# Memory tiles normed before the history and the gate weights, the low parts of the memory projection split over two engines, and the laps reordered

## The chip, the cores and the metric

The kernel runs on one core of a Trainium2 chip as one launch. The metric is device time in microseconds (us) of that launch, the median of three runs. A core has five engines that work side by side and meet at semaphores: TensorE (PE; its weight loads are shown as PEld), VectorE (DVE), ScalarE (ACT), GpSimd (POOL) and SyncE (SP), which issues DMAs. Each runs its own list of instructions in order.

## The reference

One step of a hybrid streaming encoder layer in float32. The part that matters here is its beginning: the memory tokens and the frames are normed, and the normed memory is projected to keys and values, which are outputs too.

```python
def rms_norm(x, g):
    y = xf * lax.rsqrt(jnp.mean(xf * xf, axis=-1, keepdims=True) + RMS_EPS)
    return (y * g.astype(jnp.float32)).astype(x.dtype)

def mem_kv(mem, g, w):                       # mem (1, 256, 1024), w (1024, 2048)
    kv = rms_norm(mem, g) @ w
    mk, mv = jnp.split(kv, 2, axis=-1)
...
    xn = rms_norm(x, g_mix_pre)              # 1024 prompt frames and 8 * 16 sample frames
    q, k, v, o, ig, fg, glu, xq, gates = jnp.split(xn @ w_in, IN_SPLITS, axis=-1)
```

Then come a matrix memory (mLSTM), a causal convolution over a stored history, cross-attention into the memory keys and values, a gated merge and a feed-forward block. The change touches none of that.

## The kernel before

Every product of the kernel is made in three: each operand is cut into a high part (a cast to fp32r) and a low part (the operand less its high part), and high times high, high times low and low times high are added up in PSUM. So the weights pass through two engines before TensorE may use them. A **unit** is 128 columns of a weight, 128x1024 numbers: SP loads it into `w_raw` (four buffers), ScalarE casts it to `w_hi` (two buffers, `split_hi`, L262), GpSimd subtracts to get `w_lo` (two buffers, `split_lo`, L266), and TensorE runs 24 matmuls (`use_unit`, L274). ScalarE may write `w_hi` of unit u only when TensorE has used unit u-2 (`w_used`).

The program has phases with a barrier of all engines between them (`end_phase`). The change lies in the first phase, whose five parts are `sp_norm`, `pool_norm`, `act_norm`, `pe_norm` and `dve_norm`. It has a beginning and 16 steps.

**The tiles.** Eleven tiles of 128 rows are normed and turned: 0 and 1 are the memory, 2 the sample frames, 3 to 10 the prompt. For a tile t, ScalarE squares it (`square`, L438, the sum goes to `x_ss`), VectorE makes the variance (first instruction of `scale`, L539, signals `x_var`), GpSimd takes the power -1/2 (`rstd`, L398, signals `x_rstd`), VectorE multiplies (second instruction of `scale`, L543, writes `x_s`), TensorE transposes eight blocks (`turn`, L492), VectorE applies the gain in two halves (`gain`, L549), ScalarE casts the two halves (`hi`, L444), and the low parts are made of half 0 by VectorE (`lo`, L556) and of half 1 by GpSimd (`lo`, L394). There are two buffers of `x_in` and of `x_s`, and `x_T` has one for each half.

**The beginning.** SP issues four weight units, the two memory tiles, seven vectors, the taps of the convolution, the history (`hist_in`, 960 KB) and, once GpSimd has cleared `wif`, the columns of the gate weights (L333). TensorE first transposes vectors, taps and history, then tiles 0 and 1. ScalarE casts two units and the gate weights before it squares a tile; GpSimd does low parts of the two units and of the gate weights ahead of the first `rstd`. The tiles 0, 1 and 2 are scaled and the tiles 0 and 1 gained before the steps begin.

**The steps.** Step j (`body`) runs unit j of the memory projection. In every even step one tile is handled too, with t = 3 + j/2: `scale` of tile t, `gain`, `hi` and `lo` of tile t-1 and, in step j of TensorE, `turn` of tile t-1. The result of a unit is copied from PSUM by ScalarE (`kv_T`, L460), transposed by TensorE (`kv_turn`, L502), copied by VectorE (`kv_nat`, L569) and stored. Two steps with one tile are called a pair here. `kv_steps` writes the first four steps out, and runs the other twelve as a loop of three laps of four steps, in which waits are made against registers.

Of the kernel before, what the change touches and what calls it, by code (L numbers as in the profile page):

```python
# [88 lines left out]
def hybrid_step(nc, a, o):  # L89
    ctx = ExitStack()  # L90
    with ctx:
# [228 lines left out]
        def sp_norm(sp):  # L320
            for s in range(RAW):
                load_w(sp, s, s, w_kv_v[:, :, s * P:(s + 1) * P])
            for t in range(2):
# [35 lines left out]
        def pool_norm(pool):  # L359
            steps = st["pool"] = Steps(pool, pool_steps)  # L360
            pool.sem_inc(x_lo, 1)
            steps.mark(nc.gpsimd.memset(wif[:], 0.0))
# [27 lines left out]
            def lo(t, dst):  # L390
                pool.wait_ge(x_hi, 2 * t + 2)
                d_hi, d_lo = dst(1)
                pool.wait_ge(consts_ready, 1)
                nc.gpsimd.tensor_tensor(d_lo, x_T[:, 1], d_hi.bitcast(F32), ALU.subtract).then_inc(x_lo, 1)  # L394

            def rstd(t, b):
                pool.wait_ge(x_var, t + 1)
# [26 lines left out]
        def act_norm(act):  # L424
            st["act"] = Steps(act, act_steps)
            split_hi(act, 0, 0, 0)
            split_hi(act, 1, 0, 1)
            act.wait_ge(wif_loaded, 32)
            nc.scalar.copy(wif_hi[:], wif[:]).then_inc(wif_hi_done, 1)
# [1787 lines left out]
```

## Time and profile before

| | us |
|---|---|
| median of three runs | 2942.94 (2941.67 to 2944.8) |
| span of the profiled execution | 2940.9 |
| beginning, up to the first matmul of unit 0 | 37.05 |
| first matmul of unit 0 to the first matmul of the second phase | 79.39 |
| PE busy over the span | 2737.7 (93%) |
| DVE, ACT, POOL busy over the span | 1066.5, 791.7, 1043.4 |

The span is measured from the first to the last instruction of one profiled execution; the median lies 2.0 us above it. All times in rows are us from the start of the span. In a row of the timeline the first number is the start and the second the duration; what stands in brackets is how long the engine had been idle, and what ended that. After the first phase TensorE works without a gap for a long time, so what the first phase loses or gains moves the rest.

### The profile page before, as it was taken

To read this page: it belongs to the slowest core of one execution; us is meant where nothing else is said; L and a number is where in the kernel's file an instruction comes from. 1 tells how busy PE (TensorE), PEld (TensorE's weight loads), DVE (VectorE), ACT (ScalarE), POOL (GpSimd) and SP (SyncE) were. 2 spreads that over 40 slices of the span, in tenths; PEclk is the share of its full clock that TensorE was granted. 3 is DMA by queue.
4 is the path that set the end of the run, shared out by engine and by line. 5 is a ranking of instruction groups with operands and counts; after the bars stand their busy time and mean duration, and the time that the engine had idled before them with its cause. 6 is when DMAs were issued, how large, how long until landed. Compare 5 with 4: busy or idle time off the path is not lost.

```text
span 2940.9 us, 41651 instructions
## 1 busy us (share of the span) xinstructions
PE 2737.7 (93%) x15764; PEld 2676.4 (91%) x15764; DVE 1066.5 (36%) x1418; ACT 791.7 (27%) x1172; POOL 1043.4 (35%) x525
## 2 busy tenths in 40 slices
PE   5899999999999998989988989779998899969997
PEld 5899999999999998978788879769997899969997
DVE  3320399999922222156433423231103211041101
ACT  4321111111113323044311410233333333233332
POOL 5411222222211112122011201346665566646664
PEclk9999999999999999999999989989999899989999
DMA  6422333433252232534654435424444244433442
GB/s 174 139 88 92 121 118 112 136 115 108 91 178 89 82 96 100 168 106 117 210 174 167 148 133 187 156 76 123 137 141 136 86 121 139 132 115 114 124 134 78
DMA packets 469265, 372.11 MB, mean 127 GB/s; under 512 B 13626, under 2 KB 437906, under 8 KB 469168
## 3 DMA queue, kind: packets, MB, share of 16 engines
q1 hardware_dynamic: 454264, 317.52, 35.7%
q10 hardware_dynamic: 14912, 53.48, 4.7%
q8 instruction: 46, 0.75, 0.1%
q14 instruction: 43, 0.35, 0.0%
HBM read 285.86 MB, written 85.55 MB: 126 GB/s over the span
## 4 chain that ended last, share of the span: by engine, by line
issue 47%; PE 34%; POOL 14%; DVE 2%; ACT 1%; POOLq 1%; DMA 1%; SPq 0%; DVEq 0%; ACTq 0%
PE PS L274 29%; POOL w_lo L266 12%; PE PS L1504 1%; PE PS L1523 1%; PE PS L1179 1%; PE PS L1187 1%; PE PS L1145 1%; POOL m_lo L1776 1%; DVE x_T L549 0%; POOL m_lo L1987 0%; PE PS L1152 0%; DMA stage<-in_state_conv 0%; DVE y_T L1342 0%; POOL n_r L1971 0%; PE PS L1140 0%
## 5 line engine op out<-in xcount | busy, mean ns | idle before, releaser
L266 POOL TENSOR_TENSOR w_lo<-w_raw,w_hi 128x1024 fp32r<-128x1024 f32 (+1 forms) x324 | 838.1, 2588 | 1434.0 <-ACT w_hi L262 1433.9
L262 ACT CAST w_hi<-w_raw 128x1024 fp32r<-128x1024 f32 (+1 forms) x324 | 356.0, 1099 | 1755.5 <-PE PS L274 1749.0
L274 PE MATMUL PS<-A_hi,w_hi 128*128 128x384 f32 x3024 | 752.4, 336 | 19.0 <-DVE A_lo L948 10.0
L274 PE MATMUL PS<-A_lo,w_hi 128*128 128x384 f32 x3024 | 747.8, 335 | 0.0
L274 PE MATMUL PS<-A_hi,w_lo 128*128 128x384 f32 x3024 | 747.4, 335 | 0.0
L274 PEld LDWEIGHTS PS<-A_hi,w_hi 128*128 128x128 f32 x3024 | 546.2, 189 | 22.9 <-issue 18.0
L274 PEld LDWEIGHTS PS<-A_lo,w_hi 128*128 128x128 f32 x3024 | 546.2, 188 | 0.0
L274 PEld LDWEIGHTS PS<-A_hi,w_lo 128*128 128x128 f32 x3024 | 545.8, 188 | 0.0
L274 PE MATMUL PS<-m_hi,w_hi 128*128 128x384 f32 x1248 | 428.1, 343 | 28.1 <-DVE m_lo L1776 14.9
L274 PE MATMUL PS<-m_lo,w_hi 128*128 128x384 f32 x1248 | 425.7, 341 | 0.0
L274 PE MATMUL PS<-m_hi,w_lo 128*128 128x384 f32 x1248 | 425.4, 341 | 0.0
L903 DVE SCALAR_TENSOR_TENSOR c_out<-ext,taps,c_out 128x1024 f32<-128x1024 f32 x480 | 423.9, 959 | 0.7 <-DVE c_out L903 0.7
L274 PEld LDWEIGHTS PS<-m_hi,w_hi 128*128 128x128 f32 x1248 | 236.8, 190 | 30.2 <-issue 30.0
L274 PEld LDWEIGHTS PS<-m_lo,w_hi 128*128 128x128 f32 x1248 | 236.7, 190 | 0.0
L274 PEld LDWEIGHTS PS<-m_hi,w_lo 128*128 128x128 f32 x1248 | 236.6, 190 | 0.0
L2035 DVE SCALAR_TENSOR_TENSOR ff_tmp<-ff_tmp,PS 128x384 f32<-128x384 f32 x66 | 36.6, 554 | 354.9 <-ACT ff_tmp L1904 354.9
L2018 DVE TENSOR_SCALAR nat<-PS 128x384 f32<-128x384 f32 x48 | 26.6, 557 | 349.2 <-PE PS L1845 349.0
L1027 DVE SCALAR_TENSOR_TENSOR part_out<-gate_in,PS 128x1152 f32<-128x1152 f32 x24 | 32.5, 1355 | 228.6 <-PE PS L274 228.6
L690 ACT ACTIVATE stage<-PS 128x1152 f32<-128x1152 f32 x80 | 89.9, 1124 | 0.0
L2038 DVE SCALAR_TENSOR_TENSOR ff_tmp<-ff_tmp,PS 128x384 f32<-128x384 f32 x66 | 36.6, 554 | 145.1 <-PE PS L274 145.1
L1663 POOL TENSOR_TENSOR A_lo<-xa_T,A_hi 128x512 f32 (+1 forms) x18 | 22.5, 1271 | 140.1 <-ACT A_hi L1619 140.1
L1977 POOL TENSOR_TENSOR A_lo<-ff_tmp,A_hi 128x384 f32 (+1 forms) x66 | 66.9, 1013 | 0.0
(265 smaller groups left out, 2103.5 us busy)
## 6 DMA issues: line engine op xcount, KB each, us to landing
w_raw<-in_w_ffn_in SPq DMA_DIRECT2D x132, 512.0 KB, 3.8
proj_d<-stage ACTq DMA_DIRECT2D x80, 576.0 KB, 2.8
w_raw<-in_w_in SPq DMA_DIRECT2D x80, 512.0 KB, 4.0
w_raw<-in_w_ffn_out SPq DMA_DIRECT2D x48, 704.0 KB, 4.6
gate_in<-proj_d SPq DMA_DIRECT2D x24, 576.0 KB, 6.2
part_d<-part_out SPq DMA_DIRECT2D x24, 576.0 KB, 4.5
w_raw<-in_w_branch SPq DMA_DIRECT2D x24, 512.0 KB, 4.2
w_raw<-in_w_out SPq DMA_DIRECT2D x24, 512.0 KB, 4.0
```

Source lines behind the costliest of these rows:

```text
L262: nc.scalar.copy(w_hi[:, s % SPLIT, 0:kt], w_raw[:, s, 0:kt]).then_inc(w_hi_done, 1)
L266: nc.gpsimd.tensor_tensor(w_lo[:, s % SPLIT, 0:kt], w_raw[:, s, 0:kt], w_hi[:, s % SPLIT, 0:kt].bitcast(F32), ALU.subtract).then_inc(w_lo_ ...
L274: last = nc.tensor.matmul(out, w[:, k], m(k, c), start=start and k == 0 and n == 0, stop=stop and k == kt - 1 and n == 2)
L690: nc.scalar.activation(thirds(stage[:, s % 2]), PS[:, 3 * (s % 2):3 * (s % 2) + 3, 0:TC], func, scale=scale).then_inc(p_copied, 1)
L903: steps.mark(nc.vector.scalar_tensor_tensor(out=c, in0=src, scalar=tap_scalar(w, k), in1=c, op0=ALU.mult, op1=ALU.add))
L1027: nc.vector.scalar_tensor_tensor(out=thirds(part_out[:, s % 2]), in0=thirds(gate_in[:, s % 2]), scalar=1.0, in1=PS[:, 3 * (s % 2):3 * (s % ...
L1145: last = nc.tensor.matmul(PS[:, 0, P * h:P * (h + 1)], k_in[:, b, 2 * h + z], q_in[:, b, 2 * h + z], start=z == 0, stop=z == 1)
L1179: last = nc.tensor.matmul(PS[:, 4 + h, 0:E1], q_in[:, b, 2 * h + z], C_T[:, h, z], start=z == 0, stop=z == 1)
L1187: nc.tensor.matmul(PS[:, 2 * h + z, 0:E1], kw[:, h, P * z:P * (z + 1)], v1[:, h], start=True, stop=True).then_inc(ml_upd, 1)
L1977: nc.gpsimd.tensor_tensor(l, th[:, b], h.bitcast(F32), ALU.subtract).then_inc(f_lo, 1)
L2035: nc.vector.scalar_tensor_tensor(out=th[:, b], in0=th[:, b], scalar=1.0, in1=PS[:, 2 * b, 0:TC], op0=ALU.add, op1=ALU.mult).then_inc(f_v, 1)
L2038: nc.vector.scalar_tensor_tensor(out=th[:, b], in0=th[:, b], scalar=0.5, in1=PS[:, 2 * b + 1, 0:TC], op0=ALU.mult, op1=ALU.mult).then_inc( ...
```

## The change

- `sp_norm` loads the memory tiles first, then two weight units, the vectors, taps and history, and then the other two units.
- GpSimd makes `ident` and `minus_half` alone at the start. The clearing of `wif`, the other constants and the low part of the gate weights come later, so the loads of the gate columns and of tiles 2 and 3, which stand behind them on SP, come later too.
- ScalarE squares tiles 0 and 1 first and casts the gate weights after tile 2's square. TensorE turns tiles 0 and 1 ahead of the history.
- The low part of a unit of the memory projection is made in two halves, one after the other: VectorE does k-blocks 0 to 3 (`kv_low`, signals `kv_lo`), GpSimd blocks 4 to 7 (`kv_low`, waits for `kv_lo`, signals `w_lo_done`).
- In a pair, ScalarE casts the unit before the tile's high parts, VectorE runs `kv_low`, `gain`, `lo` and then `scale` (before: `scale`, `gain`, `lo`), and GpSimd runs `rstd`, `kv_low` and then `lo`. The last lap is written out, and the loop has two laps.

VectorE, steps 2 and 3, written out: before the step begins with the scaling of tile 4 (`x_r`, `x_s`).

```order
L539 TENSOR_SCALAR x_r<-x_ss 128x1 [waits x_sq]
L543 TENSOR_SCALAR x_s<-x_in,x_r 128x1024 [waits x_turned,x_rstd]
L549 TENSOR_TENSOR x_T<-PS,cols 128x512 [waits x_lo0,x_turned]
L549 TENSOR_TENSOR x_T<-PS,cols 128x512 [waits x_lo,x_turned]
L556 TENSOR_TENSOR A_lo<-x_T,A_hi 128x4x128 [waits x_hi]
L569 COPY kv_nat<-PS 128x256 [waits kv_turned]
L569 COPY kv_nat<-PS 128x256 [waits kv_stored0,kv_turned]
```

The same place in the changed kernel:

```order
L567 TENSOR_TENSOR w_lo<-w_raw,w_hi 128x512 [waits w_hi_done]
L582 TENSOR_TENSOR x_T<-PS,cols 128x512 [waits x_lo0,x_turned]
L582 TENSOR_TENSOR x_T<-PS,cols 128x512 [waits x_lo,x_turned]
L589 TENSOR_TENSOR A_lo<-x_T,A_hi 128x4x128 [waits x_hi]
L572 TENSOR_SCALAR x_r<-x_ss 128x1 [waits x_sq]
L576 TENSOR_SCALAR x_s<-x_in,x_r 128x1024 [waits x_turned,x_rstd]
L608 COPY kv_nat<-PS 128x256 [waits kv_turned]
```

The scaling has moved from the first to the last place ahead of the copies of `kv_nat`, and the half low part, which waits for ScalarE's cast of the unit, stands first.

GpSimd, first steps of the loop's lap, before (`x_r` is the power of `rstd`, `A_lo` the tile's low part, rows without tiles are register work and waits):

```order
L398 TENSOR_TENSOR x_r<-x_r,minus_half 128x1 [waits x_var]
L391 ISA
L394 ISA [waits consts_ready,x_hi]
L394 TENSOR_TENSOR A_lo<-x_T,A_hi 128x4x128
L265 ISA
L266 TENSOR_TENSOR w_lo<-w_raw,w_hi 128x1024 [waits w_hi_done]
```

The same place in the changed kernel:

```order
L382 TENSOR_TENSOR x_r<-x_r,minus_half 128x1 [waits x_var]
L385 ISA
L386 TENSOR_TENSOR w_lo<-w_raw,w_hi 128x512 [waits kv_lo]
L376 ISA
L378 ISA [waits x_hi]
L378 TENSOR_TENSOR A_lo<-x_T,A_hi 128x4x128
```

The unit's low part now stands right behind the power, and the tile's low part behind it.

GpSimd at the beginning, before:

```order
L362 MEMSET wif 128x1024
L366 MEMSET ident 128x128 [waits pool_steps]
L366 MEMSET sel 4x512
L366 MEMSET later 128x256
L366 MEMSET own 128x8
L366 MEMSET minus_half 128x4
```

and in the changed kernel:

```order
L368 MEMSET ident 128x128
L369 MEMSET minus_half 128x4
L371 ISA [waits pool_steps]
L371 AFFINE_SELECT ident<-ident 128x128
L382 TENSOR_TENSOR x_r<-x_r,minus_half 128x1 [waits pool_steps,x_var]
L382 TENSOR_TENSOR x_r<-x_r,minus_half 128x1 [waits x_var]
L386 TENSOR_TENSOR w_lo<-w_raw,w_hi 128x512 [waits kv_lo] x2
L378 TENSOR_TENSOR mem_lo<-x_T,mem_hi 128x4x128 [waits x_hi]
L394 MEMSET wif 128x1024
```

The clearing of `wif` has moved behind two powers, two half low parts and the low part of tile 0.

```diff
@@ kv_steps
-            with eng.Fori(1, NKV // RAW) as i:
+            with eng.Fori(1, NKV // RAW - 1) as i:
                 for s in range(RAW):
                     body(RAW * i + s, i, s)
+            for s in range(RAW):
+                body(NKV - RAW + s, NKV // RAW - 1, s)
@@ sp_norm
-            for s in range(RAW):
-                load_w(sp, s, s, w_kv_v[:, :, s * P:(s + 1) * P])
             for t in range(2):
                 sp.dma_start(x_in[:, t], m_src[t]).then_inc(x_loaded[t], 16)
+            for s in range(SPLIT):
+                load_w(sp, s, s, w_kv_v[:, :, s * P:(s + 1) * P])
...
+            for s in range(SPLIT, RAW):
+                load_w(sp, s, s, w_kv_v[:, :, s * P:(s + 1) * P])
             sp.wait_ge(wif_zero, 1)
@@ pool_norm
+            def kv_low(u, s):
+                pool.wait_ge(kv_lo, u + 1)
+                nc.gpsimd.tensor_tensor(w_lo[:, s % SPLIT, KH:KT], w_raw[:, s, KH:KT],
+                                        w_hi[:, s % SPLIT, KH:KT].bitcast(F32), ALU.subtract).then_inc(w_lo_done, 1)
+
+            rstd(0, 0)
+            rstd(1, 1)
+            for s in range(SPLIT):
+                kv_low(s, s)
+            lo(0, lambda h: norm_dst(0, h))
             steps.mark(nc.gpsimd.memset(wif[:], 0.0))
-            pool.wait_ge(pool_steps, 1)
+            steps.wait()
             pool.sem_inc(wif_zero, 1)
+            lo(1, lambda h: norm_dst(1, h))
+            rstd(2, 0)
...
             def body(j, lap, s):
                 if s % 2 == 0:
                     t, b = norm_tile(lap, s)
                     rstd(t, b)
+                if isinstance(j, int) and j + SPLIT >= NKV:
+                    split_lo(pool, j + SPLIT, (s + SPLIT) % RAW)
+                else:
+                    kv_low(j + SPLIT, (s + SPLIT) % RAW)
+                if s % 2 == 0:
                     lo(t - 1, lambda h: norm_dst(t - 1, h))
-                split_lo(pool, j + SPLIT, (s + SPLIT) % RAW)
@@ act_norm
             square(0, 0, 0)
-            for t in range(1, FIRST):
-                square(t, t % 2, t // 2)
-                hi(t - 1, lambda h: norm_dst(t - 1, h)[0])
+            square(1, 1, 0)
+            split_hi(act, 0, 0, 0)
+            hi(0, lambda h: norm_dst(0, h)[0])
+            split_hi(act, 1, 0, 1)
+            hi(1, lambda h: norm_dst(1, h)[0])
+            square(2, 0, 1)
+            act.wait_ge(wif_loaded, 32)
+            nc.scalar.copy(wif_hi[:], wif[:]).then_inc(wif_hi_done, 1)
 
             def body(j, lap, s):
                 if s % 2 == 0:
                     t, b = norm_tile(lap, s)
                     square(t, b, lap + (FIRST + s // 2) // 2)
+                split_hi(act, j + SPLIT, lap + (s + SPLIT) // RAW, (s + SPLIT) % RAW)
+                if s % 2 == 0:
                     hi(t - 1, lambda h: norm_dst(t - 1, h)[0])
-                split_hi(act, j + SPLIT, lap + (s + SPLIT) // RAW, (s + SPLIT) % RAW)
@@ pe_norm
             turn(0, 0)
             turn(1, 1)
+            turn_hist()
...
             pe.wait_ge(x_lo0, FIRST)
             pe.wait_ge(x_lo, FIRST)
+            pe.wait_ge(hist_copied, 4)
@@ dve_norm
+            def kv_low(u, s):
+                dve.wait_ge(w_hi_done, u + 1)
+                nc.vector.tensor_tensor(w_lo[:, s % SPLIT, 0:KH], w_raw[:, s, 0:KH],
+                                        w_hi[:, s % SPLIT, 0:KH].bitcast(F32), ALU.subtract).then_inc(kv_lo, 1)
...
             scale(0, 0)
-            for t in range(1, FIRST):
-                scale(t, t % 2)
-                gain(t - 1, (t - 1) % 2, V_MEM)
-                lo(t - 1, *norm_dst(t - 1, 0))
+            scale(1, 1)
+            vectors()
+            kv_low(0, 0)
+            gain(0, 0, V_MEM)
+            lo(0, *norm_dst(0, 0))
+            kv_low(1, 1)
+            gain(1, 1, V_MEM)
+            lo(1, *norm_dst(1, 0))
+            copy_hist()
+            scale(2, 0)
...
             def body(j, lap, s):
                 if s % 2 == 0:
                     t, b = norm_tile(lap, s)
-                    scale(t, b)
+                if not isinstance(j, int) or j + SPLIT < NKV:
+                    kv_low(j + SPLIT, (s + SPLIT) % RAW)
+                if s % 2 == 0:
                     gain(t - 1, 1 - b, V_MIX)
                     lo(t - 1, *norm_dst(t - 1, 0))
+                    scale(t, b)
```

## Rows read from the trace of the kernel before

**Rows 1.** Busy time by stretch: start:end, length, busy per engine (instructions), clock, DMA, GB/s.

```profile
37.05:116.44 79.39, 63.66 (x483) 60.16 (x481) 29.51 (x57) 39.40 (x64) 52.59 (x32) 0.96 0.61 186
```

**Rows 2.** Timeline of PE: first matmuls of units 0 and 2, and of phase two.

```profile
37.05 0.56 PE L274 MATMUL PS<-mem_hi,w_hi 128*128 128x256 f32 x1
...
45.90 0.35 PE L274 MATMUL PS<-mem_hi,w_hi 128*128 128x256 f32 x1
...
116.44 0.87 PE L274 MATMUL PS<-A_hi,wif_hi 128*128 128x384 f32 x2 [3.16 <-POOLq L284]
```

**Rows 3.** Timeline of DVE, ACT and POOL in the loop, around one pair of steps.

```profile
67.22 0.55 POOL L398 TENSOR_TENSOR x_r<-x_r,minus_half 128x1 f32<-128x1 f32 x1
67.90 0.75 DVE L543 TENSOR_SCALAR x_s<-x_in,x_r 128x1024 f32<-128x1024 f32 x1 [1.53 <-POOL x_r L398]
68.57 1.28 DVE L549 TENSOR_TENSOR x_T<-PS,cols 128x512 f32<-128x512 f32 x2
69.38 1.22 ACT L444 CAST A_hi<-x_T 128x512 f32 x2 [3.19 <-DVE x_T L549]
70.16 0.69 DVE L556 TENSOR_TENSOR A_lo<-x_T,A_hi 128x512 f32 x1 [0.31 <-ACT A_hi L444]
...
72.04 4.70 POOL L266 TENSOR_TENSOR w_lo<-w_raw,w_hi 128x1024 fp32r<-128x1024 f32 x2
```

**Rows 4.** Timeline: a scaling and the turns after it, a cast of a unit, a turn.

```profile
25.07 0.75 DVE L543 TENSOR_SCALAR x_s<-x_in,x_r 128x1024 f32<-128x1024 f32 x1 [0.67 <-POOL x_r L398]
25.88 3.68 PE L492 MATMUL PS<-ident,x_s 128*128 128x128 f32 x16 [2.24 <-DVE x_s L543]
...
42.23 1.05 ACT L262 CAST w_hi<-w_raw 128x1024 fp32r<-128x1024 f32 x1 [3.45 <-PE PS L274]
...
45.02 1.04 PE L492 MATMUL PS<-ident,x_s 128*128 128x128 f32 x8
```

**Rows 5.** Feed-forward phase, timeline around a scaling; then line L2052: duration ns min/median/max.

```profile
1933.59 0.69 DVE L2063 TENSOR_TENSOR m_lo<-u_tail,m_hi 128x512 fp32r<-128x512 f32 x1
1934.42 0.55 POOL L1971 TENSOR_TENSOR n_r<-n_v,minus_half 128x1 f32<-128x1 f32 x1 [2.90 <-DVE n_v L2022]
1934.94 1.28 POOL L1987 TENSOR_TENSOR m_lo<-u_tail,m_hi 128x512 fp32r<-128x512 f32 x1
1935.01 1.77 DVE L2052 TENSOR_SCALAR nat<-x,n_r 128x1024 f32<-128x1024 f32 x1 [0.66 <-POOL n_r L1971]
...
L2052 DVE TENSOR_SCALAR nat<-x,n_r x9: 754/755/1776, 1927.6 to 2633.9; 128x1024 f32<-128x1024 f32 x9
```

**Rows 6.** Busy time by stretch, as in rows 1: three units, and a gap.

```profile
51.93:55.45 3.52, 1.40 (x10) 1.05 (x10) 0.69 (x2) 2.34 (x4) 3.52 (x3) 0.96 0.38 94
55.45:59.93 4.48, 4.48 (x27) 4.48 (x27) 1.71 (x4) 1.22 (x3) 2.79 (x2) 0.65 1.11 351
64.97:67.97 3.00, 3.00 (x27) 3.00 (x27) 0.22 (x2) 1.15 (x2) 2.80 (x2) 1.00 1.07 323
...
102.90:107.51 4.61, 4.61 (x27) 4.61 (x27) 1.84 (x4) 1.37 (x3) 2.79 (x2) 0.63 0.86 266
```

**Rows 7.** Timeline of POOL at the end of the first phase.

```profile
112.29 2.36 POOL L266 TENSOR_TENSOR w_lo<-w_raw,w_hi 128x1024 fp32r<-128x1024 f32 x1
...
114.89 1.43 POOL L394 TENSOR_TENSOR A_lo<-x_T,A_hi 128x512 fp32r<-128x512 f32 x1 [0.24 <-ACT A_hi L444]
```

**Rows 8.** Timeline of the beginning; last a DMA issue: KB, us to landing.

```profile
16.23 0.32 PE L472 MATMUL PS<-ident,vec_in 56*128 56x56 f32 x1 [16.23 <-DMA vec_in<-in_conv_ln_b]
...
29.41 1.06 ACT L438 ACTIVATE sq<-x_in 128x1024 f32<-128x1024 f32 x1 [0.18 <-DMA x_in<-in_x_sample]
...
30.82 0.55 POOL L398 TENSOR_TENSOR x_r<-x_r,minus_half 128x1 f32<-128x1 f32 x1 [0.25 <-DVE x_r L539]
...
35.45 1.94 PE L492 MATMUL PS<-ident,x_s 128*128 128x128 f32 x8 [5.90 <-POOL mem_lo L394]
...
x_in<-in_x_sample SPq DMA_DIRECT2D x1, 512.0 KB, 3.5
```

More of the change, by code:

```diff
@@ L301, in hybrid_step @@
         NKV = 2 * KT
+        KH = KT // 2
         N_IN = NT + MEM // P
@@ L361, in pool_norm, with lo, rstd @@
             pool.sem_inc(x_lo, 1)
+            steps.mark(nc.gpsimd.memset(ident[:], 0.0))
+            steps.mark(nc.gpsimd.memset(minus_half[:], -0.5))
+            steps.wait()
+            steps.link(nc.gpsimd.affine_select(out=ident[:], in_=ident[:], compare_op=ALU.not_equal, fill=1.0, base=0,
+                                               pattern=[[-1, P]], channel_multiplier=1))
+            pool.sem_inc(ident_ready, 1)
+            def lo(t, dst):
+                pool.wait_ge(x_hi, 2 * t + 2)
+                d_hi, d_lo = dst(1)
+                nc.gpsimd.tensor_tensor(d_lo, x_T[:, 1], d_hi.bitcast(F32), ALU.subtract).then_inc(x_lo, 1)
+            def rstd(t, b):
+                pool.wait_ge(x_var, t + 1)
+                nc.gpsimd.tensor_tensor(x_r[:, b:b + 1], x_r0[:, b:b + 1], minus_half[:, 0:1], ALU.pow).then_inc(x_rstd, 1)
+            def kv_low(u, s):
[7 more added lines that the diff above has]
+            lo(0, lambda h: norm_dst(0, h))
             steps.mark(nc.gpsimd.memset(wif[:], 0.0))
-            pool.wait_ge(pool_steps, 1)
+            steps.wait()
             pool.sem_inc(wif_zero, 1)
-            for t, v in ((ident[:], 0.0), (sel[:], 0.0), (later[:], 0.0), (own[:], 1.0), (minus_half[:], -0.5), (ln_eps[:], LN_EPS)):
+            lo(1, lambda h: norm_dst(1, h))
+            rstd(2, 0)
+            for t, v in ((sel[:], 0.0), (later[:], 0.0), (own[:], 1.0), (ln_eps[:], LN_EPS)):
                 steps.mark(nc.gpsimd.memset(t, v))
             steps.wait()
-            steps.mark(nc.gpsimd.affine_select(out=ident[:], in_=ident[:], compare_op=ALU.not_equal, fill=1.0, base=0,
-                                               pattern=[[-1, P]], channel_multiplier=1))
             steps.mark(nc.gpsimd.affine_select(out=sel[:], in_=sel[:], compare_op=ALU.not_equal, fill=1.0, base=0,
@@ L425, in act_norm @@
             st["act"] = Steps(act, act_steps)
[L426 to L429, printed above, removed]
             def square(t, b, lap):
@@ L469, in pe_norm @@
         def pe_norm(pe):
-            pe.wait_ge(consts_ready, 1)
+            pe.wait_ge(ident_ready, 1)
             pe.wait_ge(vec_loaded, 7 * 16)
@@ L476, in pe_norm, with turn_hist @@
             last.then_inc(vec_T, 1)
-            pe.wait_ge(hist_loaded, 16)
-            for n, bank in enumerate((6, 7, 4, 5)):
-                if bank == 5:
-                    pe.wait_ge(vec_copied, 1)
-                for q in range(4):
-                    k = 4 * (n % 2) + q
-                    last = nc.tensor.transpose(PS[:, bank, 120 * q:120 * (q + 1)], hist_in[:, n // 2, k * P:(k + 1) * P], ident[0:120, 0:120])
-                last.then_inc(hist_Tr, 1)
+            def turn_hist():
+                pe.wait_ge(hist_loaded, 16)
+                for n, bank in enumerate((6, 7, 4, 5)):
+                    if bank == 5:
+                        pe.wait_ge(vec_copied, 1)
+                    for q in range(4):
+                        k = 4 * (n % 2) + q
+                        last = nc.tensor.transpose(PS[:, bank, 120 * q:120 * (q + 1)], hist_in[:, n // 2, k * P:(k + 1) * P], ident[0:120, 0:120])
+                    last.then_inc(hist_Tr, 1)
             def turn(t, b):
@@ L558, in dve_norm @@
             scale(0, 0)
-            for t in range(1, FIRST):
-                scale(t, t % 2)
-                gain(t - 1, (t - 1) % 2, V_MEM)
-                lo(t - 1, *norm_dst(t - 1, 0))
+            scale(1, 1)
[8 more added lines that the diff above has]
+            scale(2, 0)
             def kv_out(e, b, before):
```

42 lines of the change are left out of this document (15 added, 27 removed).

## The prediction

> **What bounds the kernel now.** Only the first phase changes, so I read it alone, in the order in which a reader should: first the busy time by stretch, then the starts of TensorE's units, then the timelines of the engines between two units. From the first matmul of unit 0 to the second phase TensorE is busy for 63.66 of 79.39 us [rows 1]. It waits in every pair of steps, and what it waits for is GpSimd. GpSimd's round in the loop is one power (67.22), an idle stretch until the tile's low part can run, and two low parts of units (72.04, 4.70 us for both): 4.82 + 4.70 = 9.5 us for a pair [rows 3]. Six pairs, from unit 2 at 45.90 to unit 14 at 102.90, take 57.0 us, which is 9.5 each [rows 2, 6]. A unit takes 3.00 us and a turn 1.04 [rows 4, 6], so TensorE has work for about 7.4 us of those. Two of the seven pairs after the first run a slow unit, 4.48 and 4.61 us at a mean granted clock of 0.65 and 0.63; at the beginning of each the granted clock is the 1.2 GHz level, not 2.4 [rows 6]. The pair that begins at 55.45 is no longer for that (64.97 - 55.45 = 9.5): GpSimd hides the slow unit.
>
> **The beginning (term A).** The vectors that TensorE needs first come in behind 3.1 MB, four units and two tiles, and it starts at 16.23 [rows 8]. In the changed kernel 2.1 MB stand ahead of them. By bytes that is 16.23 x 4/6 = 10.8; I take 11.9, since the small loads trail. Vectors and taps are turned and copied by about 14.0 (estimate, half-speed turns and four small copies). Then a chain hangs over three engines: half a low part on VectorE (0.65, as the 0.69 of a 128x512 subtraction), the gain (0.7 to the first cast), two casts (1.2), the cast of unit 1 (1.05 + 0.1), VectorE's half (0.7), GpSimd's half (1.26, as m_lo), GpSimd's low part of tile 0 (1.25): 14.0 + 6.95 = 20.95 [rows 3 to 5]. Behind these on GpSimd stands the clearing of `wif`, 1 us, and behind that clearing wait SP's two gate loads and the sample tile: 22.0, plus 1.0 for two issues, plus 3.5 for the tile [rows 8], plus 0.3 behind the gate packets: 26.8. From a square to the power 1.41, from the power to the scaling 0.6, from it to the turn 0.81, from the turn to unit 0 1.60 [rows 4, 5, 8]: 26.8 + 4.4 = **31.2**, against 37.05. So A = -5.9. If the vectors came at 10.8 it would be -7; if the gate loads held SP for two more us, -4. Ends: -9 and -2. The constants and the gate weights' low part, moved behind the power of tile 2, lie under unit 0, since GpSimd's next power cannot come before unit 0 has ended. The history's turns and copies lie under the load of the sample tile.
>
> **The pairs (terms B and C).** Here the new order makes a ring. VectorE's step now begins with a half low part that waits for ScalarE's cast of unit j+2, which waits until TensorE has used unit j. Behind this half on VectorE stand the gain and low part of tile t-1 and then the scaling of tile t; and unit j+2 stands on TensorE behind the turn of tile t. Before, the scaling came first and did not depend on unit j. So from the end of unit j to the start of unit j+2 run, one after the other: to the cast 0.1, cast and hand-over 1.12, half low part 0.63, gain to cast 0.81, cast to VectorE's low part 0.78 [rows 3, 4], that to the power 0.83, power to scaling 0.6 to 0.68 [rows 3, 5], scaling to turn 0.81, turn 0.9 to 1.0 [rows 4]. The sum is 6.6 (6.3 where the steps are written out, where hand-overs are shorter by 0.1; 6.8 in the loop). GpSimd's half low part, 1.26, is not in this sum: it can run while the tile is scaled and turned. But it does not only hide, it gets in the way. It stands right behind the power, its input has been ready for three us, and so it starts as the power ends, a trace ahead of the scaling. The feed-forward phase has the same two neighbours: power to 1934.97, GpSimd's 128x512 subtraction from 1934.94 to 1936.22, VectorE's 128x1024 scaling from 1935.01, and that scaling takes 1.77 us instead of 0.75 [rows 5]. It happened in three of nine, each time that GpSimd was 0.06 or 0.07 us ahead; the other six took 0.75. So the scaling ends 0.95 later (0.55 after GpSimd's half), and a pair takes 3.0 + 6.6 + 0.95 = 10.5 us instead of 9.5.
>
> The Trainium skill, "SBUF — State Buffer", section "Who interferes with whom", says the same as a rule and speaks against this change: VectorE in a two-port mode and GpSimd share a pair of ports, and whoever issues second is blocked until the first has finished. The trace agrees (1.77 against 0.75). Without it terms B and C below would be smaller by 0.95 for each pair.
>
> **B**, the first pair: unit 0 runs at the low clock as before (45.90 - 37.05 = 8.85 held 5.0 of it). Now 5.0 + 6.3 + 0.95 = 12.3, since nothing of tile 3 is done ahead any more: B = +3.4. **C**, six further pairs at 10.5 instead of 9.5: +6.0. Ends: without the collision B is 2.5 and C 0.6; with loop hand-overs 0.3 dearer C is 8.
>
> **The clock (term D).** TensorE now has, between unit j+1 and the turn, only one pair of small transposes in about 3.4 us. Before, in a like stretch ahead of the slow unit at 55.45, it was busy for 1.40 of 3.52 us, and then the granted clock fell [rows 6]. I expect a fall in nearly every pair. Its price is no longer hidden, as unit and turn lie on the ring: a slow unit costs 1.5 to 1.6 (4.48 and 4.61 against 3.00), and a slow turn 0.9 more (1.94 against 1.04) [rows 4, 6, 8]. I take 1.8 for each of seven units: D = +12.6. Ends: 0, and 7 x 2.5 = 17.
>
> The Trainium skill, "TensorE: Matmul & The Clock Gate", section "HAM oscillation — how this bites in real kernels", has it that a wait of that kind that comes in every round lets every round start cold. By the rows of before alone, two falls in seven, D would be 3. No run here shows yet which of the two holds for this ring.
>
> **The end (term E).** From unit 14 to the second phase it took 116.44 - 102.90 = 13.5. The last two units' low parts stay whole, so after unit 14 come: cast and the high part of tile 9 (to 1.7), its low part, variance and power (to 3.1), a whole low part of 2.35, in which the last scaling is caught, and which it ends 0.5 behind, GpSimd's low part of tile 9 (1.25) and the second whole low part (2.35): 9.55. From the end of that one (114.65 in the trace) to the second phase 1.8 [rows 2, 7]. So 3.0 + 11.35 = 14.3: E = +0.8 (0 to 3).
>
> **The sum.** -5.9 + 3.4 + 6.0 + 12.6 + 0.8 = +16.9. The second phase begins at about 133 instead of 116.4, and nothing after it changes. Against the profiled execution that is 2940.9 + 16.9 = 2957.8, and the runs lie 2.0 above their span: **2960**.
>
> **The rivals.** (1) The clock holds better: collisions as forecast, but two falls of seven as before, D = 3: +7.3, 2950. For it: the other five pairs before kept their clock although TensorE waited in each. Against: in the new ring it waits longer and does less meanwhile. (2) No collision, because in the loop register work stands between power and half low part and the scaling gets ahead. Then pairs have 6.6, idle stretches are shorter, and with four falls at 1.6: -5.9 + 2.5 + 0.6 + 6.4 - 0.1 = +3.5, 2946. Against it: in the loop two low parts follow each other without a gap (4.70 for two of 2.35). (3) The other side, faster: the ring is cheaper than its rows. If hand-overs between VectorE and its neighbours shrink as its halves follow each other, so that a pair takes 8.3 us, C = -7, without falls: -5.9 + 1 - 7 - 0.1 = -12, 2931. It decides from a ring of about 5.3 instead of 7.55 us on; only the loss of a cast and of the collision would give that, and both are in every pair. (4) The change does not bring the memory tiles forward, as the sample tile waits behind the gate loads: A near -1, and with the rest 2965.
>
> **How the numbers follow.** Forecast 0.62 (2953 to 2967), rival 1 0.13, rival 2 0.11, rival 3 and other gains 0.10, rival 4 0.04. The range leaves out rival 3, the lower half of rival 2 and a few above: 2945 to 2967. A measurement of this kernel tells about 0.2% (5.9 us) from no change, so 2948.8 and 2937.1 are the limits: slower 0.75 (forecast, rival 4 and most of rival 1), same 0.14 (rival 2, the rest), faster 0.11.
>
> **What would show it.** Unit 0 near 31 (A). Unit starts 12 to 13 us apart in the pairs, with slow units of some 4.5 us (C, D); 10.5 apart with units of 3.0 would be rival 1. Scalings of 1.7 us with GpSimd's half low part beginning just ahead of each (collision); 0.75 is rival 2. Second phase near 133 (sum). Wrong would be the forecast if a turn starts before the cast of the next unit has been through VectorE: then there is no ring.

## The result and the profile after

The changed kernel takes 2956.57 us (median of four, 2956.21 to 2960.88) against 2942.66 (four runs beside it): a ratio of 1.0051, 95% interval 1.0037 to 1.0066. It is slower by 13.9 us. The profiled execution took 2956.49, its span is 2954.7 against 2940.9. The second phase begins at 131.30 instead of 116.44, 14.86 later; 1.0 of that comes back behind it (2823.4 us from there to the end against 2824.4), and I did not follow that up.

Busy time by stretch of the changed kernel, columns as in [rows 1]: the whole loop, the six pairs from unit 2 to unit 14, then single units, a gap with its turn, a piece of a slow unit, and the gaps ahead of units 10 and 14.

```profile
31.79:131.30 99.51, 69.97 (x482) 66.50 (x480) 52.67 (x73) 39.91 (x64) 44.21 (x36) 0.84 0.52 158
44.27:116.16 71.89, 53.16 (x362) 50.57 (x361) 37.73 (x55) 29.80 (x47) 28.25 (x24) 0.85 0.55 167
...
44.27:49.31 5.04, 5.04 (x29) 5.04 (x27) 0.35 (x2) 0.00 (x0) 1.28 (x1) 0.57 0.64 189
57.40:61.09 3.69, 3.69 (x29) 3.69 (x27) 0.26 (x1) 0.00 (x0) 1.28 (x1) 0.80 0.74 210
68.59:73.19 4.60, 4.60 (x30) 4.60 (x28) 1.03 (x2) 0.40 (x2) 1.43 (x2) 0.63 0.76 203
116.16:119.23 3.07, 3.07 (x30) 3.07 (x28) 2.32 (x4) 0.22 (x2) 1.53 (x2) 1.00 0.75 193
...
65.70:69.10 3.40, 1.35 (x12) 1.36 (x13) 3.25 (x3) 2.47 (x4) 3.04 (x3) 1.00 0.28 95
69.20:72.40 3.20, 3.20 (x17) 3.20 (x17) 0.42 (x2) 0.00 (x0) 1.28 (x1) 0.50 0.84 219
...
88.00:92.52 4.52, 1.28 (x10) 1.05 (x11) 3.53 (x6) 3.14 (x6) 3.32 (x3) 1.00 0.18 63
111.98:116.16 4.18, 1.28 (x11) 1.05 (x11) 3.43 (x6) 3.20 (x6) 3.23 (x3) 1.00 0.20 71
```

Against [rows 1] TensorE is busy 6.3 us longer for the same matmuls (69.97 against 63.66) and waits 13.8 us longer (29.54 against 15.73). The longer busy time is the clock: in 65.70 to 69.10 it was busy for 1.35 of 3.40 us, and from 69.20 to 72.40 the granted clock is 0.50, the 1.2 GHz level. The first units of six pairs in a row (units 2, 4, 6, 8, 10 and 12) begin at that level and last 0.6 to 2.0 us longer than the 3.00 of [rows 6]; the seventh (unit 14, 116.16) runs in 3.07 at 1.00.

The longer wait is the ring. Timeline of the changed kernel from the end of unit 4, which releases the cast of unit 6, to the turn ahead of unit 6:

```profile
61.13 1.05 ACT L262 CAST w_hi<-w_raw 128x1024 fp32r<-128x1024 f32 x1 [4.17 <-PE PS L274]
62.21 0.69 DVE L567 TENSOR_TENSOR w_lo<-w_raw,w_hi 128x512 fp32r<-128x512 f32 x1 [4.54 <-ACT w_hi L262]
62.82 1.28 DVE L582 TENSOR_TENSOR x_T<-PS,cols 128x512 f32<-128x512 f32 x2
63.63 1.21 ACT L458 CAST A_hi<-x_T 128x512 f32 x2 [1.46 <-DVE x_T L582]
64.43 0.69 DVE L589 TENSOR_TENSOR A_lo<-x_T,A_hi 128x512 f32 x1 [0.33 <-ACT A_hi L458]
...
65.27 0.55 POOL L382 TENSOR_TENSOR x_r<-x_r,minus_half 128x1 f32<-128x1 f32 x1 [6.58 <-DVE x_r L572]
...
65.78 1.27 POOL L386 TENSOR_TENSOR w_lo<-w_raw,w_hi 128x512 fp32r<-128x512 f32 x1
65.85 1.75 DVE L576 TENSOR_SCALAR x_s<-x_in,x_r 128x1024 f32<-128x1024 f32 x1 [0.66 <-POOL x_r L382]
...
67.75 1.09 PE L514 MATMUL PS<-ident,x_s 128*128 128x128 f32 x8 [2.13 <-DVE x_s L576]
```

GpSimd's half low part starts 0.07 us ahead of the scaling, the scaling takes 1.75 instead of the 0.75 of [rows 3], and TensorE's turn waits 2.13 for it. Unit 6 starts at 68.59, 7.50 behind the end of unit 4 (61.09), where the working had 7.55. All scalings, with duration in ns (min, median, max):

```profile
L576 DVE TENSOR_SCALAR x_s<-x_in,x_r x11: 753/1748/2828, 6.5 to 122.4; 128x1024 f32<-128x1024 f32 x11
```

The longest stands in the end of the phase, behind a whole low part:

```profile
122.28 2.35 POOL L266 TENSOR_TENSOR w_lo<-w_raw,w_hi 128x1024 fp32r<-128x1024 f32 x1
122.35 2.83 DVE L576 TENSOR_SCALAR x_s<-x_in,x_r 128x1024 f32<-128x1024 f32 x1 [0.66 <-POOL x_r L382]
...
126.48 1.93 SPq L350 DMA_DIRECT2D out_p_mem_v<-kv_nat  x2
127.58 0.42 DVE L608 COPY kv_nat<-PS 128x256 f32<-128x256 f32 x1 [1.73 <-DMA out_p_mem_v<-kv_nat]
127.92 1.28 DVE L582 TENSOR_TENSOR x_T<-PS,cols 128x512 f32<-128x512 f32 x2
...
129.92 1.26 POOL L378 TENSOR_TENSOR A_lo<-x_T,A_hi 128x512 fp32r<-128x512 f32 x1 [1.31 <-ACT A_hi L458]
```

VectorE is held until 125.2, its copies of the output follow late, the last copy waits 1.73 for the store that frees its buffer, and the last gain stands behind that copy.

### The profile page after: what moved, and what is told of

It is laid out like the page before. It is cut to its first block, busy times and chain, and to the rows that moved or that the text cites. A ratio compares the mean times of both kernels' runs of the same rounds, so it can differ in the third digit from the quotient of the medians.

```text
span 2954.7 us, 41574 instructions
## 1 busy us (share of the span) xinstructions
PE 2742.7 (93%) x15764; PEld 2681.7 (91%) x15764; DVE 1090.4 (37%) x1434; ACT 791.8 (27%) x1172; POOL 1029.9 (35%) x525
## 4 chain that ended last, share of the span: by engine, by line
issue 47%; PE 34%; POOL 14%; DVE 2%; ACT 1%; POOLq 1%; DMA 0%; ACTq 0%; DVEq 0%; SPq 0%
PE PS L274 29%; POOL w_lo L266 11%; PE PS L1221 1%; PE PS L1229 1%; PE PS L1547 1%; PE PS L1566 1%; PE PS L1187 1%; POOL m_lo L1818 1%; POOL m_lo L2029 0%; PE PS L1182 0%; PE PS L1203 0%; DVE y_T L1384 0%; POOL n_r L2013 0%; PE PS L1194 0%; POOL A_lo L378 0%
## 5 line engine op out<-in xcount | busy, mean ns | idle before, releaser
L266 POOL TENSOR_TENSOR w_lo<-w_raw,w_hi 128x1024 fp32r<-128x1024 f32 (+1 forms) x308 | 800.3, 2598 | 1429.5 <-ACT w_hi L262 1429.4
```

The costliest lines, as they stand in the source:

```text
L266: nc.gpsimd.tensor_tensor(w_lo[:, s % SPLIT, 0:kt], w_raw[:, s, 0:kt], w_hi[:, s % SPLIT, 0:kt].bitcast(F32), ALU.subtract).then_inc(w_lo_ ...
```

## Experiments

All kernels are built from the changed one unless the text says otherwise. The table splits each profiled execution as the prediction does: first matmul of unit 0; unit 0 to unit 2; unit 2 to unit 14 (six pairs, with the mean granted clock in it); unit 14 to the second phase. Ratios are to the kernel before, in runs on the same chip.

| kernel | unit 0 | first pair | six pairs (clock) | end | median us | ratio, 95% |
|---|---|---|---|---|---|---|
| before | 37.05 | 8.85 | 57.00 (0.97) | 13.54 | 2942.66 | |
| changed | 31.79 | 12.48 | 71.89 (0.85) | 15.14 | 2956.57 | 1.0037 to 1.0066 |
| e1 half after scaling | 31.13 | 11.47 | 62.56 (0.93) | 14.69 | 2945.81 | 1.0001 to 1.0019 |
| e2 scale first | 31.17 | 9.23 | 50.22 (1.00) | 13.37 | 2930.15 | 0.9941 to 0.9971 |
| e3 filled gap | 31.27 | 12.10 | 62.85 (1.00) | 15.12 | 2947.72 | 1.0007 to 1.0026 |
| e4 beginning alone | 31.14 | 10.06 | 57.04 (0.97) | 13.55 | 2938.43 | 0.9977 to 0.9995 |
| e5 laps alone | 37.24 | 12.18 | 74.92 (0.81) | 15.14 | 2965.63 | 1.0055 to 1.0089 |
| e6 earlier beginning | 28.92 | 8.86 | 50.22 (1.00) | 13.32 | 2928.55 | 0.9934 to 0.9967 |
| e7 scale first, whole | 31.81 | 8.69 | 56.33 (0.94) | 13.63 | 2931.53 | 0.995 to 0.9978 |
| e8 e1 and e3 together | 31.24 | 11.72 | 59.79 (1.00) | 14.72 | 2943.49 | 0.9992 to 1.0011 |
| e9 sample tile first | 24.75 | 9.11 | 50.31 (1.00) | 13.30 | 2927.16 | 0.9926 to 0.9953 |
| e10 ScalarE's order | 32.66 | 10.06 | 59.16 (0.94) | 14.63 | 2945.31 | 0.9996 to 1.0014 |

**Beginning and laps apart (e4, e5).** e4 takes the changed beginning and the laps of the kernel before; e5 the reverse. On VectorE that is, in e4:

```diff
-                if not isinstance(j, int) or j + SPLIT < NKV:
-                    kv_low(j + SPLIT, (s + SPLIT) % RAW)
                 if s % 2 == 0:
+                    scale(t, b)
                     gain(t - 1, 1 - b, V_MIX)
                     lo(t - 1, *norm_dst(t - 1, 0))
-                    scale(t, b)
```

> The beginning of the changed kernel with the laps of the kernel before (scaling first, whole low parts on GpSimd, tile's parts before the unit's). Theory: the beginning brings unit 0 forward by 5.3 us and the laps keep that: 2936 to 2939. Rival (the beginning's gain is given back, since the second memory pair or the sample tile is late): 2941 to 2944.

> The kernel before's beginning with the changed laps (shared low parts, gains and half low parts ahead of the scaling). Theory, that the loss lies wholly in the laps: the changed kernel's own stretches give +3.6 for the first pair, +14.9 for the six after it and +1.6 at the end, +20.1 on 2942.7, so 2960 to 2965; the first unit starts at 37.0 as in the kernel before, pairs last 11 to 13, and the clock falls in most of them. Rival, that the laps are neutral and the changed beginning drives the loops into the slow rhythm: 2943, pairs at 9.5.

Measured 2938.43 and 2965.63: -4.9 and +22.6 against the kernel before on the same chips. The beginning is a gain and the laps are the whole loss. The theory of e4 held (2936 to 2939); e5 came out just above its range (2960 to 2965). (Together the two make 17.7, not 13.9. Six units start slow in e5 as in the changed kernel, but units 8 and 10 last 4.97 and 5.09 against 3.62 and 4.62, and its profile is the longest of its four executions.) e5's six pairs are the slowest of all, at the lowest clock:

```profile
49.42:124.34 74.92, 55.72 (x362) 53.12 (x361) 37.71 (x55) 29.73 (x47) 28.21 (x24) 0.81 0.52 160
```

So the slow rhythm does not come from the new beginning: the rival of e5 falls.

**The clock by itself (e3).** Idle matmuls of the memory tile stand in TensorE's wait, eight ahead of the transposes of `kv_T` and twelve behind them, into a bank that the next turn overwrites.

```diff
+                if s % 2 == 1:
+                    t, b = norm_tile(lap, s - 1)
+                    pe.wait_ge(x_gained, 2 * (t - 2) + 1)
+                    fill(8, b)
                 if not isinstance(j, int) or j > 0:
                     kv_turn(j - 1, (s + 1) % 2)
+                if s % 2 == 1:
+                    fill(12, b)
```

> The changed kernel with idle matmuls on TensorE in the wait of each pair: 8 ahead of the transposes of the odd step and 12 behind, 256 columns each, into a bank that the next turn overwrites. The output isn't affected. Theory (the ring is 10.5 us at full clock, the rest of a pair is slow units and turns): the clock holds, units take 3.0 and pairs 10.5 to 10.7, second phase at about 122.5, 2946 to 2949. Rival (the slow units lie beside another wait that is as long): pairs stay at 12 and the time within 2 us of 2956.5, or the added matmuls come on top.

Measured 2947.72. Six pairs of the filled kernel, by stretch:

```profile
43.37:106.22 62.85, 58.23 (x483) 55.81 (x481) 38.68 (x55) 30.12 (x49) 28.77 (x25) 1.00 0.63 191
```

At a clock of 1.00 throughout, as the theory had it, six pairs take 62.85 instead of 71.89. The price of the falls is 9.04, one and a half us each for six; the medians lie 8.85 apart. Its turns still wait for the scaling, so the idle matmuls do not stand in the ring themselves:

```profile
84.53 1.09 PE L514 MATMUL PS<-ident,x_s 128*128 128x128 f32 x8 [0.65 <-DVE x_s L586]
```

**The blocked scaling (e1, e8).** GpSimd's half low part waits until the scaling has ended.

```diff
                     rstd(t, b)
+                    pool.wait_ge(x_scaled, t + 1)
```

> The changed kernel, in which GpSimd's half low part also waits until VectorE has scaled the tile, so the two can't collide. Theory (ring with a collision in it): scalings fall from 1.75 to 0.75 us, the half then ends about 2.2 us after the power instead of the scaling's 1.8 and the turn's 2.8, so unit j+2 starts some 0.6 us earlier in each of seven pairs: 2951 to 2954 against 2956.5, units 11.4 instead of 12.0 apart on average. Rival (the collision lies beside something else): the scalings get short and the time stays within 1 us of 2956.5.

> The changed kernel with idle matmuls in TensorE's wait, which kept the clock up, and with GpSimd's half low part held back until the scaling has been issued and ended, which kept the pair of VectorE and GpSimd from blocking each other. It measures the blocked scaling by itself, at full clock. Theory: the blocked scaling costs its 1.0 us on the chain of the sample or prompt tile, some 0.5 to 1.0 of a pair of 10.5; pairs at 9.5 to 10.0, the time 2941 to 2945. Rival, that at full clock it is hidden behind the high and low parts of the weights, and the loss came by the clock alone: pairs at 10.3 to 10.6, 2946 to 2948.

e1 measured 2945.81, 10.8 below the changed kernel, where the theory had 2951 to 2954. Its scalings are all short again:

```profile
L577 DVE TENSOR_SCALAR x_s<-x_in,x_r x11: 753/753/978, 6.6 to 111.3; 128x1024 f32<-128x1024 f32 x11
```

But the mean granted clock of its six pairs also rose, from 0.85 to 0.93. e8 tells the two apart, since there the clock is 1.00 with and without the block: six pairs fall from 62.85 (e3) to 59.79 (e8).

```profile
42.96:102.75 59.79, 58.38 (x480) 55.84 (x481) 34.20 (x55) 30.12 (x49) 28.63 (x25) 1.00 0.66 201
```

Holding GpSimd's half back gives 3.06 in six pairs, 0.51 each, which is half of the scaling's own 1.0 and inside the theory of e8. It is less than the block costs, since the remedy has a price too: held back, GpSimd's half now ends last at the next unit. Timeline of e8 around unit 10:

```profile
80.59 0.75 DVE L587 TENSOR_SCALAR x_s<-x_in,x_r 128x1024 f32<-128x1024 f32 x1 [0.67 <-POOL x_r L382]
...
81.52 1.28 POOL L386 TENSOR_TENSOR w_lo<-w_raw,w_hi 128x512 fp32r<-128x512 f32 x1 [0.97 <-DVE x_s L587]
...
81.62 1.03 PE L515 MATMUL PS<-ident,x_s 128*128 128x128 f32 x8
...
82.85 0.39 PE L274 MATMUL PS<-mem_hi,w_hi 128*128 128x256 f32 x1 [0.20 <-POOL w_lo L386]
```

The scaling ends at 81.34. In e3 the turn begins at least 0.06 behind the end of its scaling, and the unit 0.85 behind the start of the turn (84.53 to 85.38). By that, unit 10 could have begun at 82.25, 0.6 earlier than it did. (The idle matmuls held the turn until 81.62 here, but the unit waited for the half anyway.) The same working over the six pairs of e8 gives 9.4 for a pair through the scaling instead of 9.97 (an estimate). Against the 10.5 of e3 the block then costs about its whole 1.0, and the hold gives half of that away again.

Of the 9.33 that e1 gained in its six pairs, 3.1 are the hold, as in e8, and the other 6.3 are then the clock: three of its units (2, 6 and 12) begin slow instead of six.

**The order on VectorE (e2).** The scaling goes back to the front of VectorE's step; all else stays as changed.

```diff
+                    scale(t, b)
                 if not isinstance(j, int) or j + SPLIT < NKV:
                     kv_low(j + SPLIT, (s + SPLIT) % RAW)
                 if s % 2 == 0:
                     gain(t - 1, 1 - b, V_MIX)
                     lo(t - 1, *norm_dst(t - 1, 0))
-                    scale(t, b)
```

> The changed kernel with one move: in a pair VectorE scales tile t first, then makes its half low part, gain and the tile's low part. Theory (ring): the scaling and the turn no longer hang on unit j, the path from unit j to unit j+2 is cast, two halves, some 3.3 us, shorter than the other unit, and TensorE's own work of 7.4 us or ScalarE's 6.5 sets the pair: 7.5 to 8.5 us instead of 12, the granted clock holds, 2925 to 2932. Rival (the two halves and the added hand-over are what costs, or the clock falls whatever the order): 2950 or more.

Measured 2930.15, as the theory had it and faster than both kernels, with six pairs in 50.22, 8.37 each. One pair of e2:

```profile
59.86 0.55 POOL L382 TENSOR_TENSOR x_r<-x_r,minus_half 128x1 f32<-128x1 f32 x1 [0.35 <-DVE x_r L572]
59.87 1.05 ACT L262 CAST w_hi<-w_raw 128x1024 fp32r<-128x1024 f32 x1 [0.27 <-PE PS L274]
60.54 0.76 DVE L576 TENSOR_SCALAR x_s<-x_in,x_r 128x1024 f32<-128x1024 f32 x1 [0.76 <-POOL x_r L382]
61.21 0.69 DVE L567 TENSOR_TENSOR w_lo<-w_raw,w_hi 128x512 fp32r<-128x512 f32 x1
...
61.98 1.28 POOL L386 TENSOR_TENSOR w_lo<-w_raw,w_hi 128x512 fp32r<-128x512 f32 x1 [1.57 <-DVE w_lo L567]
```

The scaling runs beside ScalarE's cast of the next unit, so it is off the ring, and GpSimd's half, which waits for VectorE's half behind the scaling, cannot get ahead of it. One move of one line is worth 26.4 us here.

**What else in the laps matters (e7, e10).** e7 is e2 with the low parts whole on GpSimd (first edit, GpSimd's step; VectorE's half goes out too). e10 is e4 with ScalarE's new order alone (second edit, ScalarE's step).

```diff
-                if isinstance(j, int) and j + SPLIT >= NKV:
-                    split_lo(pool, j + SPLIT, (s + SPLIT) % RAW)
-                else:
-                    kv_low(j + SPLIT, (s + SPLIT) % RAW)
+                split_lo(pool, j + SPLIT, (s + SPLIT) % RAW)
```

```diff
+                split_hi(act, j + SPLIT, lap + (s + SPLIT) // RAW, (s + SPLIT) % RAW)
                 if s % 2 == 0:
                     hi(t - 1, lambda h: norm_dst(t - 1, h)[0])
-                split_hi(act, j + SPLIT, lap + (s + SPLIT) // RAW, (s + SPLIT) % RAW)
```

> The run with the scaling first, with the low part of every weight unit in the loops whole on GpSimd again (2.3 us in one instruction) instead of two halves one after the other (0.7 on VectorE, then 1.3 on GpSimd). Theory, that the order on VectorE and ScalarE made the gain and the division hardly any: the halves follow one another, 1.96 against 2.34, so 0.4 for each unit at most, pairs at 8.2 to 9.2, the time 2930 to 2934. Rival, that the division carries the gain: pairs at 9.5 as in the kernel before, 2937 to 2939.

> The changed beginning with the kernel before's laps, in which ScalarE alone takes the changed order: the weight unit's high part ahead of the tile's two high parts. The run with this and GpSimd's whole low part ahead of the tile's low part gave 2931.5, that with neither 2938.4. Theory, that the earlier high part is what shortens the pair, as everything of the next unit follows from it: 2931 to 2934. Rival, that GpSimd's order is what counts, since the low part of the weights still stands behind the tile's low part there: 2936 to 2939.

e7 measured 2931.53, and its interval overlaps that of e2: dividing the low part has no measurable gain at the median. Its single times lie further apart (2928.88 to 2937.01, e2 2928.57 to 2931.19), and its profile, one of the longer executions, shows a reason: now a whole low part can get ahead of the scaling. (The row of e7 in the table is of that execution; its pairs of 9.39 lie outside the theory's 8.2 to 9.2, its median inside.)

```profile
44.88 2.40 POOL L266 TENSOR_TENSOR w_lo<-w_raw,w_hi 128x1024 fp32r<-128x1024 f32 x1
44.94 2.88 DVE L573 TENSOR_SCALAR x_s<-x_in,x_r 128x1024 f32<-128x1024 f32 x1 [2.04 <-POOL x_r L382]
```

e10 measured 2945.31, above the ranges of the theory and of the rival: ScalarE's order alone is no gain against e4's 2938.43, but a loss. GpSimd is still last there, and now its unit's low part stands behind a tile's low part that comes later, as ScalarE's casts for it do:

```profile
67.09 1.22 ACT L452 CAST A_hi<-x_T 128x512 f32 x2 [0.30 <-DVE x_T L576]
68.52 1.27 POOL L376 TENSOR_TENSOR A_lo<-x_T,A_hi 128x512 f32 x1 [3.04 <-ACT A_hi L452]
69.76 4.70 POOL L266 TENSOR_TENSOR w_lo<-w_raw,w_hi 128x1024 fp32r<-128x1024 f32 x2
...
72.16 0.38 PE L274 MATMUL PS<-mem_hi,w_hi 128*128 128x256 f32 x1 [1.84 <-POOL w_lo L266]
```

Of the 6.9 between e10 and e4 its six pairs hold 2.1 and the end 1.1; its later first unit (1.5) and the part behind the second phase's start (2.6) lie where nothing was edited. With both orders, ScalarE giving the unit's high part first and GpSimd taking the unit's low part first, the gain is 6.9 by the medians (e4 to e7; e7's last lap is written out, too). GpSimd's order alone was not run, so it is not shown that it takes both.

**A beginning without queues (e6, e9).** Both are e2 with an earlier sample tile. In e6 its load goes ahead of the gate loads; in e9 also ahead of the history and of the third and fourth unit, which there stand behind the gate loads too. The edit is that of e9 on SyncE, against e2; where the other engines' steps went, the expectations say.

```diff
+            load_x(2, 0, s_src)
             sp.dma_start(hist_in, a["state_conv"][0].rearrange("(g b) r c -> (b r) g c", g=2)).then_inc(hist_loaded, 16)
-            for s in range(SPLIT, RAW):
-                load_w(sp, s, s, w_kv_v[:, :, s * P:(s + 1) * P])
             sp.wait_ge(wif_zero, 1)
...
+            for s in range(SPLIT, RAW):
+                load_w(sp, s, s, w_kv_v[:, :, s * P:(s + 1) * P])
-            load_x(2, 0, s_src)
             load_x(3, 1, x_src[0])
```

> The changed kernel with the scaling first on VectorE, and a beginning in which nothing of the sample tile waits for the gate weights: GpSimd zeroes their tile at once, SyncE loads the sample tile and the first prompt tile ahead of them, ScalarE forms both high parts of the first two weight units ahead of the first memory tile's, VectorE and GpSimd their low parts as soon as these are there, and VectorE scales the sample tile ahead of the four history copies. Theory, that the first unit waits for the sample tile's chain (load at 22.5, square 26.3, scaling 28.3, turn 29.6 in the run with the scaling first): the first unit at 21 to 24 instead of 31.2, the time 2920 to 2924. Rival, that the second pair takes the gain back, since its prompt tiles, high parts or weights are not there earlier: the first unit early, the first pairs longer, 2926 to 2930.

> The run with the scaling first and the earlier beginning, with the sample tile's load now ahead of the history load and of the third and fourth weight unit's loads too (it stood 6.1 us in SyncE's queue behind them, and landed 11.1 us after its issue), its square ahead of the first memory tile's high parts on ScalarE, and its scaling on VectorE between the first memory tile's gains and low part. Theory, that loads in a queue that has no room were what held the sample tile: the first unit at 20.5 to 23 instead of 28.9, the pairs unchanged at 8.2 to 8.9, the time 2920 to 2923. Rival, that the same bytes have to come in any order, so that the history, the third weight unit or the first prompt tile is what is late next: the first unit at 22 or later and the first two pairs longer by what it gained, 2925 to 2929.

e6 measured 2928.55, not the 2920 to 2924 of its theory, as unit 0 starts at 28.92. (That is in the rival's range, but not for the rival's reason: the first pair is no longer than in e2.) Timeline of SyncE in e6:

```profile
8.70 1.87 SPq L255 DMA_DIRECT2D w_raw<-in_w_mem_kv  x2
10.61 6.08 SPq L340 DMA_DIRECT2D x_in<-in_x_sample  x1
```

Behind the history (0.96 MB) and two units of 0.5 MB, the issue of the sample load stands for 6.08 us. In e9 it goes out at 8.22 in 0.49, and it is the third and fourth unit that stand, for 6.21. Unit 0 starts at 24.75, 4.2 earlier; I had expected 20.5 to 23. Its median is 2927.16, only 1.4 below e6. The rival's range holds that, but the rival's longer first pairs are not there (9.11 against 8.86 in e6): in the profiled executions e9 takes 2828.8 us behind the second phase's start and e6 2825.2. (e9's is the longest of its five, 2923.53 to 2928.0.) One place where that is lost is a granted clock that falls in e9 at 1423; in e6 a like, shorter wait leaves it at 1.00. The first two rows are e9, the other two e6:

```profile
1420.00:1423.00 3.00, 0.96 (x9) 0.97 (x10) 1.94 (x6) 0.28 (x1) 0.00 (x0) 0.99 0.66 194
1423.50:1426.00 2.50, 2.50 (x8) 1.95 (x7) 0.86 (x2) 0.48 (x2) 0.00 (x0) 0.50 0.20 67
...
1423.00:1425.40 2.40, 1.13 (x9) 0.73 (x8) 1.85 (x6) 0.00 (x0) 0.00 (x0) 1.00 0.94 285
1425.40:1430.00 4.60, 4.60 (x29) 4.08 (x28) 1.97 (x4) 1.94 (x6) 0.00 (x0) 1.00 0.49 134
```

e9 is the fastest kernel here, at 0.994 of the one before; e6 and e2 cannot be told from it with certainty.

## Why the prediction was right, and where its sizes were off

Time (2956.57 against 2960), sign and mechanism held. By its own terms:

- **A**, -5.9 forecast, -5.26 measured (37.05 to 31.79). The vectors were there as the bytes had it (10.83), the taps 1.9 later; from there the chain ran nearly as written: clearing of `wif` at 20.84 (forecast 20.95; the parts of that sum make 20.91), the sample tile's square at 26.96 (26.8). Its load goes out at 22.92: behind the gate loads, but not later than before, where it went out at 25.85. The rows below are the timeline of the changed kernel's beginning.

```profile
10.83 0.32 PE L492 MATMUL PS<-ident,vec_in 56*128 56x56 f32 x1 [10.83 <-DMA vec_in<-in_conv_ln_b]
12.69 0.68 PE L495 MATMUL PS<-ident,tap_in 124*128 124x124 f32 x2 [1.53 <-DMA tap_in<-in_conv_w]
...
20.84 0.96 POOL L394 MEMSET wif<- 128x1024 f32 x1
...
21.88 0.99 SPq L339 DMA_DIRECT2D wif<-in_w_in  x2
...
22.92 0.66 SPq L343 DMA_DIRECT2D x_in<-in_x_sample  x1
...
26.96 1.06 ACT L453 ACTIVATE sq<-x_in 128x1024 f32<-128x1024 f32 x1 [4.60 <-DMA x_in<-in_x_sample]
```

- **B**, +3.4 forecast, +3.63 measured (44.27 - 31.79 = 12.48 against 8.85). That it fits so closely is luck: unit 1 starts 4.33 behind unit 0 where the working had 5.0, and the turn ahead of unit 2 ran slow (1.97), a price that the working had put under D.
- **C**, +6.0 forecast, +5.85 measured: six pairs at full clock are 62.85 in e3, 10.5 each as forecast, against 57.00. The split inside it holds as far as e8 shows it: about 9.4 for the pair without the block where the working had 9.6, and about 1.0 for the block where it had 0.95 (estimates, see e8). That holding GpSimd back gives only 0.51 of this was in no part of the working.
- **D**, +12.6 forecast, +9.04 measured: the term that was mis-sized. "I take 1.8 for each of seven units" failed twice. Six of the seven units fell, the last did not; and each fall cost 1.5, because the prices of a slow turn and of the slow unit behind it do not add up. The turns ahead of units 4, 8 and 12 took 1.97 instead of 1.09, and these units then lost only 0.6 to 0.7; units 6 and 10, behind a turn at full speed, lost 1.6, and unit 2, whose slow turn lies in the first pair, 2.0. The Trainium skill, "TensorE: Matmul & The Clock Gate", section "HAM oscillation — how this bites in real kernels", has every round start cold when each wait is long enough. Here the trace agrees for six rounds of seven, and the count by the rows of before (two of seven) was far off.
- **E**, +0.8 forecast, +1.60 measured. I followed GpSimd's chain, and it came as written: its last whole low part ended at 128.61, 12.45 behind unit 14 (12.55 in the working). What ended last was VectorE's, held by the blocked scaling of 2.83 (expected) and then by a copy that waited 1.73 for a store (not in the working); GpSimd's last low part waited 1.31 for it.

The sum is +14.86 against +16.9. The step "nothing after it changes" is off by 1.0.

Of the rivals, the first (two falls) and the second (no collision) did not happen; e1 makes the second true by force and takes 2945.81, where its price was 2946. That the two numbers agree is luck: the price had pairs of 9.6 and four falls, the runs 9.97 (e8) and three falls (e1). The third, the faster side, named the right condition, "a ring of about 5.3 instead of 7.55": e2 gets there (8.37 for a pair, 5.4 behind the first unit's 3.0) by taking the scaling off the ring, though "only the loss of a cast and of the collision would give that" overlooked this way. The fourth fell, as unit 0 shows; yet the sample tile does wait behind the gate loads, and e6 and e9 start earlier without that.

Not settled: why unit 14 kept its clock and unit 10 did not, though the gaps ahead of them look alike (busy for 1.28 of 4.18 and 1.28 of 4.52 us); what sets e2's pair of 8.37, above TensorE's own 7.4; and why the part behind the second phase's start varies between 2823.4 (changed) and 2828.8 (e9), beyond the one fall that I found.

## What to carry to other kernels

Before a wait is put at the head of an engine's step, list what stands behind it on that engine and who needs that: here a scaling that needed nothing of the loop was put behind work that waits for TensorE, and TensorE waits for the scaling. When work is divided between VectorE and GpSimd, order it so that GpSimd's instruction depends on the VectorE instruction that it could otherwise get ahead of, and look at whether GpSimd's instruction then ends last (it did in e8, and half of the gain was gone; it did not in e2). Price a longer wait of TensorE with the clock that it may lose: in e1 a remedy worth 3.1 us at full clock gave back 9.3.

## What the runs showed of the hardware that I had not expected

- Holding GpSimd's half back gained 9.33 us in six pairs where the clock was falling (e1), and 3.06 where it was not (e8).
- The block scales with GpSimd's instruction: a scaling of 0.75 takes 1.75 behind a 128x512 low part and 2.88 behind a 128x1024 one (e7). The Trainium skill, "SBUF — State Buffer", section "Who interferes with whom", lets the second issuer wait for the whole instruction; the trace agrees to about 0.2 us, as in e7 the scaling ended at 47.82, 0.54 us after GpSimd's end at 47.28, and alone it takes 0.75.
- A load's issue can stand for 6 us on SyncE (e6, e9), and with it every load and wait behind it, though the issue of the same load takes 0.49 in e9, where the history and the two units stand behind it.
